# A hybrid decoder step on one core: the first softmax scores of a tile one query feature later

## The chip, the cores and the metric
One Trainium2 chip, one of its cores. The metric is the device time of one execution in microseconds, the median of several runs; lower is better. The engines are TensorE (PE, and PEld for its weight loads), VectorE (DVE), ScalarE (ACT), GpSimd (POOL) and SyncE (SP, which issues the DMAs here).

## The reference
One layer of a decoder with two groups of heads side by side, for a prompt of 2048 tokens and 8 single new tokens. A row norm of x is projected by one combined matrix of width 2832 into:

- a gated linear attention group: 4 heads with keys of 64 and values of 128, a decay from a low-rank gate (rank 16), a per-token recurrence evaluated in chunks;
- a sliding-window softmax group: 8 query heads of width 64 that share 2 key and value heads, window 128, with one learned sink logit per head.

```
proj = einsum('bld,de->ble', rmsnorm(x), w_in)      # gq gk gv g_gate g_low sq sk sv s_gate
o_gla = rmsnorm(gla_scan(gq, gk, gv, log_sigmoid(g_low @ w_gate_up + b) / 16))
s     = q . k / 8, banded: query block i reads key blocks i-1 and i
p     = softmax([s, sink])[..., :-1];   o_swa = p @ v
y     = rmsnorm(x + concat(o_gla * silu(g_gate), o_swa * silu(s_gate)) @ w_out)
```

The outputs are y for the prompt and for the new tokens, the recurrent states, and the last window of keys and values.

## The kernel before, in words
The prompt is cut in 16 tiles of 128 tokens. Every float32 product of the projections is made of three half-precision matmuls (high x high, high x low, low x high; lines L616, L617, L618 in `split_product`). A preamble scales and splits the weights; then a loop over tiles 0 to 14 (`body`) runs on every engine, each with an order written out by hand; tile 15 and the 8 new tokens come behind it. TensorE's body for tile t works ahead: it projects tile t+1 while it finishes the attention of tile t. Tile 0 has an order of its own. The order for t = 1 to 14:

1. `proj(nxt, "sq")`: the window queries of tile t+1, four features of 128 columns, each 8 x 3 matmuls of 128 rows by 128 columns. Between two of them stands `first_scores(t)`, which is `scores(t, 0)`: the scores of units 0 and 1 (12 matmuls of 64 rows, L721).
2. `scores(t, 1)`: units 2 and 3. Then `leaf_scores(t)`, the projection "sklow" (key, value and low-rank part), half of "gv", `values(t, 0)` and `values(t, 1)` (probabilities times values), the rest of "gv", the level scores, `turn_keys`, `turn_low`, `values(t, 2)`, `values(t, 3)`.
3. Part of "gg", the gate, the linear attention's output and state, the rest of "gg", "sg", "gqk" of tile t+2, and the output projection of tile t (L616 to L618 on w_out), with a broadcast `bc(t + 3)` behind its second half's fifth chunk.

PSUM banks are handed out by rings of two. In the ring of the attention each tile fills s0, s1, s2, s3, L1, L2, y0, y1 in turn; a unit waits until the unit two places before it is freed. So s0 and s1 wait for y0 and y1 of the tile before (freed by VectorE's `residual`, L1806), and s2 and s3 wait for s0 and s1, which VectorE frees with the last instruction of `row_max(t, 0)` and `row_max(t, 1)` (L1694 to L1701: two small copies, a predicated copy, two reductions). In the ring of the projections "gv" waits for "sq", which VectorE frees at L1572.

What follows the scores: ScalarE takes the exponential (L1237) and the high half (L1256), VectorE the low half (`rows_lo`, L1719); SyncE then issues a DMA transpose per unit (`turn_prob_rows`, L544), for units 2 and 3 only after TensorE's `values` of units 0 and 1 are over; VectorE masks the transposed tile (`mask_older`, L1725), and `values(t, u)` waits for that. VectorE's order in a tile is row_max 0 and 1, the mean of the final norm (L1812), rows_lo 0 and 1, take_sq (L1572), row_max 2 and 3, mask_older 0 and 1, rows_lo 2 and 3, take_kv, the leaves, the softmax denominators, mask_older 2 and 3, the levels, and then `take_z`, which waits for TensorE.

Of the kernel before, what the change touches and what calls it, by code (L numbers as in the profile page):

```python
# [160 lines left out]
def hymba_step_kernel(nc, xT_d, xq_d, xsT_d, xs_d, w_d, gin_d, gout_d, wgu_d, bg_d, sink_d, normf_d, normfT_d,  # L161
                      state_d, kcT_d, vc_d, sinks_s_d, ident_d, tri_d, lvl_d, leafscan_d, band_d, older_d, window_d,
                      y_d, ys_d, Sp_d, kp_d, vp_d, Ss_d, ksT_d, vs_d):
    with ExitStack() as ctx:
# [446 lines left out]
        def _(pe):  # L611
# [17 lines left out]
            def features(t, bank, at_, c0, ntile, step=P):  # L629

                n = t.tokens
                for f in range(ntile):
                    c = c0 + f * P
                    mm = split_product(bank[:, at_ + f * step:at_ + f * step + n],
                                       [(w_hi[:, d, c:c + P], w_lo[:, d, c:c + P],
                                         u_hi[:, t.p, d, 0:n], u_lo[:, t.p, d, 0:n]) for d in range(DT)])
                return mm

            def rows(t, bank, at_, c0, width, d0=0, d1=DT):

                n = t.tokens
                return split_product(bank[0:n, at_:at_ + width],
                                     [(u_hi[:, t.p, d, 0:n], u_lo[:, t.p, d, 0:n],
                                       w_hi[:, d, c0:c0 + width], w_lo[:, d, c0:c0 + width]) for d in range(d0, d1)],
                                     start=d0 == 0, stop=d1 == DT)

            def proj_rest(t, name, d0, d1=DT):

                mm = rows(t, pj.bank(name, t), 0, COL[name], 512, d0, d1)
                if d1 == DT:  # L650
                    mm.then_inc(pj.full, 1)
# [33 lines left out]
            def proj(t, name, d1=DT, between={}):  # L685
                if t.static and t.off <= 1:
                    i = PREP.index([g for g, _ in GROUPS].index(name))
                    pe.wait_ge(w_lo_done, i + 1)
                pj.wait_free(pe, name, t)
                dve_u.wait(pe, "lo", t)  # L690
                bank = pj.bank(name, t)
                if name in ("gqk", "sq"):
                    for f in range(4):
                        mm = features(t, bank, f * P, COL[name] + f * P, 1)
                        for step, i in between.get(f, ()):
                            step(i)
                elif name == "sklow":
                    features(t, bank, 0, COL[name], 1)
                    mm = rows(t, bank, P, COL[name] + P, P + RANK)
                else:  # L700
                    mm = rows(t, bank, 0, COL[name], 512, 0, d1)
                if d1 == DT:
                    mm.then_inc(pj.full, 1)

            def scores(t, pair):

                units = [f"s{2 * pair + h}" for h in range(KVH)]
                for name in units:  # L710
                    at_ring.wait_free(pe, name, t)
                if pair == 0:
                    pj.wait_freed(pe, "sq", t)
                    pj.wait_freed(pe, "sklow", t)
                    if not (t.static and t.off == 0):
                        win_kept.wait(pe, "win", t + -1)
                for i in range(2):
                    for step, (lq, lk) in enumerate(((0, 0), (0, 1), (1, 0))):
                        for h, name in enumerate(units):
                            r = h * HD  # L720
                            mm = nc.tensor.matmul(at_ring.bank(name, t)[:, i * 2 * P:(i + 1) * 2 * P],  # L721
                                                  q16[r:r + HD, t.p, lq, 2 * pair + i, :], k16[r:r + HD, t.p, lk, :],
                                                  start=step == 0, stop=step == 2)
                            if i == 1 and step == 2:
                                mm.then_inc(at_ring.full, 1)
# [4 lines left out]
            def turn_probs(t, u):  # L730
                name = f"pt{u}"
                tr.wait_free(pe, name, t)
                act_w.wait(pe, f"p{u}", t)
                bank = tr.bank(name, t)
                for i in range(2):
                    tp = nc.tensor.transpose(bank[:, i * P:i * P + P], PR[:, u % 2, i, :], ident[:, :])
                tp.then_inc(tr.full, 1)

            def values(t, u):
                if u == 0:  # L740
                    if t.static and t.off == 0:
                        pe.wait_ge(z_taken, 1)
                    else:
                        dve_o.wait(pe, "sg", t + -1)
                if u == 0:
                    dve_v.wait(pe, "vl", t)
                dve_p.wait(pe, f"k{u}", t)
                h = u % 2
                for i in range(2):
                    c = (u // 2 * 2 + i) * P + h * HD  # L750
                    v = v16[:, t.p, :, h * HD:h * HD + HD]
                    mm = split_product(accS[:, c:c + HD],
                                       [(PT[:, u % 2, m, 0, i, :], PT[:, u % 2, m, 1, i, :], v[:, 2 * m], v[:, 2 * m + 1])
                                        for m in range(2)])
                mm.then_inc(pe_pv.sem, 1)
# [32 lines left out]
            def leaf_scores(t):  # L788

                ring = leaf_ring(t)  # L790
                for h in range(2):
                    ring.wait_free(pe, f"leaf{h}", t)
                dve_g.wait(pe, "leaf", t)
                for f in range(FT):
                    for h in range(2):
                        r = h * DK
                        mm = nc.tensor.matmul(ring.bank(f"leaf{h}", t)[:, f * P:f * P + P],  # L797
                                              EX[r:r + DK, S_LEAFK, f, :], QL[r:r + DK, f, :], start=True, stop=True)
                        if f == FT - 1:
                            mm.then_inc(ring.full, 1)  # L800
# [220 lines left out]
            def body(t):  # L1021
                nxt = t + 1
                early = t.static and t.off == 0
                if early:
                    turn_probs(t, 0)
                    turn_probs(t, 1)
                    scores(t, 1)
                    proj(nxt, "gv")
                    proj(t, "gg")
                    values(t, 0)  # L1030
                    values(t, 1)
                    leaf_scores(t)
                    turn_probs(t, 2)
                    turn_probs(t, 3)
                    proj(t, "sg")
                    values(t, 2)
                    level_scores(t, "L1", 0)
                    values(t, 3)
                    level_scores(t, "L2", 2)
                    turn_keys(t)  # L1040
                    turn_low(t)
                else:
                    proj(nxt, "sq", between={0: [(first_scores, t)]})
                    scores(t, 1)
                    leaf_scores(t)
                    proj(nxt, "sklow")
                    proj(nxt, "gv", 4)
                    values(t, 0)
                    values(t, 1)
                    proj_rest(nxt, "gv", 4)  # L1050
                    level_scores(t, "L1", 0)
                    level_scores(t, "L2", 2)
                    turn_keys(t)
                    turn_low(t)
                    values(t, 2)
                    values(t, 3)
                proj(nxt, "gg", 3)
                gate_up(t)
                gla_out(t)
                state_update(t)  # L1060
                proj_rest(nxt, "gg", 3)
                if early:
                    proj(nxt, "sg", 5)
                    turn_out(t, 0)
                    turn_out(t, 1)
                    proj_rest(nxt, "sg", 5)
                    out_proj(t, 0, 0, 5)
                    bc(t + 2)
                    out_proj(t, 0, 5)
                    out_proj(t, 1)  # L1070
                    proj(t + 2, "gqk")
                    bc(t + 3)
                else:
                    proj(nxt, "sg")
                    proj(t + 2, "gqk")
                    out_proj(t, 0)
                    out_proj(t, 1, 0, 5)
                    if t.n + 3 <= NT:
                        bc(t + 3)
                    out_proj(t, 1, 5)  # L1080

            iterations(pe, body)
            t = Tile(NT - 1)
# [1291 lines left out]
```

## Time and profile before
| | |
|---|---|
| median of 3 runs | 874.51 us (873.07 to 875.18) |
| the profiled execution | 876.44 us, its span 874.7 us |
| TensorE busy (matmuls) | 851.1 us, 97% |
| VectorE, ScalarE, GpSimd busy | 676.9 us, 389.8 us, 77.5 us |
| mean granted TensorE clock | 0.973 |
| one tile of the loop | 48.09 us (scores of tile 2 at 180.92, of tile 3 at 229.01) |

Busy time of an engine is the time in which it has an instruction in work. Matmuls are pipelined and overlap in the records, so their starts say more than their lengths. Where a row ends in brackets, the engine was idle before it for so long and what is named released it.

### The profile page before, as it was taken

To read this page: it belongs to the slowest core of one execution; us is meant where nothing else is said; L and a number is where in the kernel's file an instruction comes from. 1 tells how busy PE (TensorE), PEld (TensorE's weight loads), DVE (VectorE), ACT (ScalarE), POOL (GpSimd) and SP (SyncE) were. 2 spreads that over 40 slices of the span, in tenths; PEclk is the share of its full clock that TensorE was granted. 3 is DMA by queue.
4 is the path that set the end of the run, shared out by engine and by line. 5 is a ranking of instruction groups with operands and counts; after the bars stand their busy time and mean duration, and the time that the engine had idled before them with its cause. 6 is when DMAs were issued, how large, how long until landed. Compare 5 with 4: busy or idle time off the path is not lost.

```text
span 874.7 us, 22036 instructions
## 1 busy us (share of the span) xinstructions
PE 851.1 (97%) x8842; PEld 591.3 (68%) x8842; DVE 676.9 (77%) x2211; ACT 389.8 (45%) x1008; POOL 77.5 (9%) x117
## 2 busy tenths in 40 slices
PE   7898999999999999999999999999999999998997
PEld 5885657676667667576766676675767666764775
DVE  5899787968878787869788787878696887775854
ACT  4556453544444444445444443444454444443411
POOL 0041010101001010101010010101010100101310
PEclk6999999999999999999999999999999999999977
DMA  9922001413122132315132221313141312214033
GB/s 370 394 112 74 25 25 26 121 25 100 35 60 86 38 97 49 99 25 121 25 89 47 60 82 42 97 42 104 27 121 20 110 31 33 63 19 122 3 106 128
DMA packets 75747, 71.22 MB, mean 81 GB/s; under 512 B 63807, under 2 KB 65271, under 8 KB 74622
## 3 DMA queue, kind: packets, MB, share of 16 engines
q1 hardware_dynamic: 75358, 69.75, 27.4%
q8 instruction: 70, 1.15, 0.6%
q14 instruction: 31, 0.25, 0.1%
q10 hardware_dynamic: 288, 0.07, 0.0%
HBM read 44.33 MB, written 10.78 MB: 63 GB/s over the span
## 4 chain that ended last, share of the span: by engine, by line
PE 88%; issue 4%; DVE 4%; DMA 2%; ACT 1%; SPq 0%; POOL 0%; POOLq 0%; DVEq 0%
PE bank L616 25%; PE bank L618 24%; PE bank L617 24%; PE bank L811 3%; PE bank L721 3%; PE bank L670 2%; PE bank L833 2%; PE bank L837 2%; PE bank L848 1%; PE bank L797 1%; DMA w_out_hi<-in_w 1%; DVE w_in_hi_lo L1875 1%; PE bank L626 1%; DMA ogT_lo<-x_rows 1%; DVE xT L1528 0%
## 5 line engine op out<-in xcount | busy, mean ns | idle before, releaser
L616 PE MATMUL bank<-u_hi,w_in_hi_lo 128*128 128x128 f16 (+1 forms) x1288 | 210.3, 215 | 2.9 <-DVE w_in_hi_lo L1875 2.6
L618 PE MATMUL bank<-u_hi,w_in_hi_lo 128*128 128x128 f16 (+1 forms) x1288 | 210.0, 215 | 0.0
L617 PE MATMUL bank<-u_lo,w_in_hi_lo 128*128 128x128 f16 (+1 forms) x1288 | 210.0, 215 | 0.0
L616 PE MATMUL bank<-w_in_hi_lo,u_hi 128*128 128x512 f16 (+3 forms) x528 | 175.1, 341 | 3.6 <-issue 3.6
L618 PE MATMUL bank<-w_in_hi_lo,u_lo 128*128 128x512 f16 (+3 forms) x528 | 175.5, 341 | 0.0
L617 PE MATMUL bank<-w_in_hi_lo,u_hi 128*128 128x512 f16 (+3 forms) x528 | 175.3, 341 | 0.0
L616 PEld LDWEIGHTS bank<-u_hi,w_in_hi_lo 128*128 128x128 f16 x1288 | 124.2, 98 | 12.1 <-issue 3.2
L617 PEld LDWEIGHTS bank<-u_lo,w_in_hi_lo 128*128 128x128 f16 x1288 | 124.1, 98 | 3.0
L618 PEld LDWEIGHTS bank<-u_hi,w_in_hi_lo 128*128 128x128 f16 x1288 | 124.0, 98 | 0.0
L616 PE MATMUL bank<-w_out_hi,ogT_hi 128*128 128x512 f16 x256 | 98.3, 384 | 2.5 <-DMA ogT_lo<-x_rows 2.0
L617 PE MATMUL bank<-w_out_lo,ogT_hi 128*128 128x512 f16 x256 | 98.2, 384 | 0.0
L618 PE MATMUL bank<-w_out_hi,ogT_lo 128*128 128x512 f16 x256 | 98.0, 383 | 0.0
L618 PEld LDWEIGHTS bank<-w_in_hi_lo,u_lo 128*128 128x128 f16 (+1 forms) x528 | 51.6, 98 | 46.9 <-issue 0.8
L616 PEld LDWEIGHTS bank<-w_in_hi_lo,u_hi 128*128 128x128 f16 (+1 forms) x528 | 51.7, 98 | 45.3 <-issue 7.4
L617 PEld LDWEIGHTS bank<-w_in_hi_lo,u_hi 128*128 128x128 f16 (+1 forms) x528 | 51.7, 98 | 38.5 <-issue 0.8
L1237 ACT ACTIVATE flex<-flex,win_stat 128x128 f32<-128x128 f32 x128 | 49.9, 390 | 45.3 <-DVE win_stat L1701 45.3
L1725 DVE TENSOR_TENSOR flex<-flex,older_slot 128x512 f16<-128x512 f16 x56 | 22.7, 423 | 35.1 <-DMA flex<-win_p_rows_hi_lo 35.1
L2228 POOL TENSOR_TENSOR flex<-flex,win_stat 128x512 f32<-128x512 f32 x16 | 16.7, 1043 | 372.3 <-DVE win_stat L1737 345.9
L1296 ACT ACTIVATE ogT_hi<-flex 128x1024 bf16<-128x1024 f32 x16 | 16.9, 1056 | 73.3 <-DVE flex L1806 73.3
L1701 DVE CUSTOM_DVE_ANT_0 flex<-bank,band_bf,neg_sinks 128x128 f32<-128x128 f32 x128 | 47.0, 405 | 0.0
L618 PEld LDWEIGHTS bank<-w_out_hi,ogT_lo 128*128 128x128 f16 x256 | 25.3, 99 | 31.0 <-issue 1.4
L616 PEld LDWEIGHTS bank<-w_out_hi,ogT_hi 128*128 128x128 f16 x256 | 25.8, 101 | 29.8 <-issue 4.3
(310 smaller groups left out, 1663.7 us busy)
## 6 DMA issues: line engine op xcount, KB each, us to landing
xT<-in_xT SPq DMA_DIRECT2D x16, 512.0 KB, 3.3
x_rows<-in_xq SPq DMA_DIRECT2D x16, 512.0 KB
flex<-in_w SPq DMA_DIRECT2D x4, 2048.0 KB, 9.9
flex<-in_xq SPq DMA_DIRECT2D x16, 512.0 KB, 4.1
out_y<-flex SPq DMA_DIRECT2D x16, 512.0 KB, 3.7
w_out_lo<-in_w SPq DMA_DIRECT2D x2, 2048.0 KB, 11.9
w_out_hi<-in_w SPq DMA_DIRECT2D x1, 2048.0 KB, 9.9
w_out_hi<-in_w SPq DMA_DIRECT2D x1, 1088.0 KB, 7.5
```

Of the source, the lines that this page charges most:

```text
L616: nc.tensor.matmul(out, a_hi, b_hi, start=start and i == 0, stop=False)
L617: nc.tensor.matmul(out, a_hi, b_lo, start=False, stop=False)
L618: mm = nc.tensor.matmul(out, a_lo, b_hi, start=False, stop=stop and i == last)
L670: mm = nc.tensor.matmul(out[0:w, 0:w], top[:, d, c:c + w], top[:, d, c:c + w], start=d == 0 and c == 0, stop=d == DT - 1 and (c, w) == blo ...
L721: mm = nc.tensor.matmul(at_ring.bank(name, t)[:, i * 2 * P:(i + 1) * 2 * P], q16[r:r + HD, t.p, lq, 2 * pair + i, :], k16[r:r + HD, t.p, l ...
L811: mm = nc.tensor.matmul(bank[:, c:c + P], EX[:, l0 + l, f, :], QE[:, l0 + l, f].rearrange("p h c -> p (h c)"), start=True, stop=True)
L833: nc.tensor.matmul(accG[:, f * 2 * DV:(f + 1) * 2 * DV], EX[:, S_INTER, f, :], S_bd[:, f].rearrange("p h c -> p (h c)"), start=f == 0, sto ...
L837: mm = nc.tensor.matmul(accG[:, h * DV:h * DV + DV], AT[:, h, :], gv[:, t.p, h * DV:h * DV + DV], start=False, stop=h == HG - 1, skip_grou ...
L1237: e = nc.scalar.activation(PR[:, u % 2, i, :], PR[:, u % 2, i, :], ACT.Exp, scale=-1.0, bias=wst[:, 0, k:k + 1], accum_out=wst[:, 1, k:k + 1])
L1296: nc.scalar.activation(junk[0:n, :], xres[0:n, :], ACT.Square, accum_out=hst[0:n, 0:1]).then_inc(act_o.sem, 1)
L1701: m = V.tensor_tensor_reduce(PR[:, u % 2, i, :], bank[:, i, P:2 * P], band[:, first], nsig[:, :], nsink[:, k:k + 1], ALU.add, ALU.min, wst ...
L1725: V.tensor_tensor(PT[:, u % 2, 1].rearrange("p l h c -> p (l h) c"), PT[:, u % 2, 0].rearrange("p l h c -> p (l h) c"), bcast(older16[:, : ...
```

## The change
`first_scores(t)` moves from behind feature 0 to behind feature 1 of the next tile's query projection, in tiles 1 to 14 on TensorE. No other engine's order changes and no instruction is added or dropped. The broadcast behind five chunks of the output projection is in both kernels.

```diff
@@ -1040,7 +1040,7 @@
                     turn_keys(t)
                     turn_low(t)
                 else:
-                    proj(nxt, "sq", between={0: [(first_scores, t)]})
+                    proj(nxt, "sq", between={1: [(first_scores, t)]})
                     scores(t, 1)
                     leaf_scores(t)
                     proj(nxt, "sklow")
```

## Rows read from the trace of the kernel before

**Rows 1.** The page, part 1: busy us, share of the span, instructions.
```profile
PE 851.1 (97%) x8842; PEld 591.3 (68%) x8842; DVE 676.9 (77%) x2211; ACT 389.8 (45%) x1008; POOL 77.5 (9%) x117
```

**Rows 2.** The waits of TensorE: us in total, times, longest.
```profile
PE bank L616 <- issue: 3.6, 1, 3.6
...
PE bank L721 <- DVE flex L1806: 1.0, 1, 1.0
...
PE bank L616 <- ACT gla_k L1164: 0.3, 1, 0.3
```

**Rows 3.** The chain that ended last, tiles 2 and 3: start, us.
```profile
180.92 0.76 PE bank L721 x12
...
229.01 0.76 PE bank L721 x12
```

**Rows 4.** Timeline of TensorE's weight loads, tile 6, from 373.3 us.
```profile
373.40 0.10 PEld L618 LDWEIGHTS bank<-u_hi,w_in_hi_lo 128*128 128x128 f16 x1
373.60 0.55 PEld L721 LDWEIGHTS bank<-win_k_hi_lo,win_q_hi_lo 64*128 64x128 f16 x12
...
374.44 0.10 PEld L618 LDWEIGHTS bank<-u_hi,w_in_hi_lo 128*128 128x128 f16 x1
...
378.29 0.10 PEld L618 LDWEIGHTS bank<-u_hi,w_in_hi_lo 128*128 128x128 f16 x1
378.49 0.55 PEld L721 LDWEIGHTS bank<-win_k_hi_lo,win_q_hi_lo 64*128 64x128 f16 x12
```

**Rows 5.** Timeline of VectorE, tile 6, from 369 us.
```profile
372.58 0.74 DVE L1806 SCALAR_TENSOR_TENSOR flex<-bank,row_unscale,flex 128x512 f32<-128x512 f32 x1
374.47 0.15 DVE L1694 COPY win_stat<-neg_sinks 128x1 f32<-128x1 f32 x1 [1.14 <-PE bank L721]
...
376.64 0.41 DVE L1701 CUSTOM_DVE_ANT_0 flex<-bank,band_bf,neg_sinks 128x128 f32<-128x128 f32 x1
...
379.35 0.69 DVE L1572 SCALAR_TENSOR_TENSOR win_q_hi_lo<-bank,win_q_hi_lo 128x512 f16<-128x512 f32 x1 [0.39 <-ACT win_q_hi_lo L1180]
...
382.45 0.76 DVE L1725 TENSOR_TENSOR flex<-flex,older_slot 128x512 f16<-128x512 f16 x2
...
384.01 0.42 DVE L1719 SCALAR_TENSOR_TENSOR win_p_rows_hi_lo<-flex,win_p_rows_hi_lo 128x256 f16<-128x256 f32 x1 [0.47 <-ACT win_p_rows_hi_lo L1256]
...
388.11 0.42 DVE L1725 TENSOR_TENSOR flex<-flex,older_slot 128x512 f16<-128x512 f16 x1 [1.42 <-DMA flex<-win_p_rows_hi_lo]
389.43 0.42 DVE L1725 TENSOR_TENSOR flex<-flex,older_slot 128x512 f16<-128x512 f16 x1 [0.90 <-DMA flex<-win_p_rows_hi_lo]
```

**Rows 6.** Timeline of all engines at tile 15's first scores, behind the loop.
```profile
806.10 0.75 DVE L1806 SCALAR_TENSOR_TENSOR flex<-bank,row_unscale,flex 128x512 f32<-128x512 f32 x1 [4.42 <-PE bank L618]
...
806.92 0.14 PEld L721 LDWEIGHTS bank<-win_k_hi_lo,win_q_hi_lo 64*128 64x128 f16 x4 [1.45 <-DVE flex L1806]
```

**Rows 7.** Timeline of all engines at the second scores of tile 14.
```profile
761.75 0.41 DVE L1701 CUSTOM_DVE_ANT_0 flex<-bank,band_bf,neg_sinks 128x128 f32<-128x128 f32 x1
...
763.61 0.12 PEld L721 LDWEIGHTS bank<-win_k_hi_lo,win_q_hi_lo 64*128 64x128 f16 x4
```

**Rows 8.** Timeline of TensorE's matmuls, tile 6, from 378 us.
```profile
382.55 0.38 PE L616 MATMUL bank<-w_in_hi_lo,u_hi 128*128 128x512 f16 x1
...
385.14 0.19 PE L616 MATMUL bank<-win_v_hi_lo,flex 128*128 128x64 f16 x1
...
385.49 0.19 PE L616 MATMUL bank<-win_v_hi_lo,flex 128*128 128x64 f16 x1
...
390.84 0.19 PE L616 MATMUL bank<-win_v_hi_lo,flex 128*128 128x64 f16 x1
```

**Rows 9.** The waits of VectorE and of SyncE's queue.
```profile
DVE flex L1725 <- DMA flex<-win_p_rows_hi_lo: 35.1, 30, 2.5
DVE win_stat L1694 <- PE bank L721: 16.2, 15, 1.2
...
SPq L544 <- PE bank L618: 33.2, 14, 2.4
```

## The prediction, made before the result was known
> **What bounds the kernel now.** I read the page first. TensorE has work in 97% of the span, VectorE in 77% and ScalarE in 45% [rows 1]. So a change inside the tile loop costs or gives only what it does to TensorE's idle time. The view of waits then says where TensorE is idle. It has 13 kinds of wait; the longest is 3.6 us and the shortest 0.3 us, and together they make 3.6 + 2.6 + 2.0 + 2.0 + 1.9 + 1.4 + 1.1 + 1.0 x 4 + 0.5 + 0.3 = 19.4 us. The only one on the line of the scores (L721) is 1.0 us [rows 2], and it lies at 806.9 us, where tile 15 is scored behind the loop [rows 6], a place that the change does not touch. In the chain of work the scores of every tile stand on TensorE, and the first ones repeat every 48.09 us (180.92, then 229.01) [rows 3]. The loop's tiles are therefore TensorE's own work from end to end, and there is no stall in them at the scores that a change of place could remove.
>
> **What the change does on TensorE.** Nothing is added, removed or resized. In tiles 1 to 14, feature 1 of the next tile's query (24 matmuls with their weight loads) now runs before the first scores instead of after them. A feature's loads go from 374.44 to 378.29 in 69 steps, 0.0558 us each, so a feature is 24 x 0.0558 = 1.34 us [rows 4]. There is a small toll at each entry from the features to the scores: from the last load of the features (373.40) to the first load of the scores (373.60) it is 0.20 us where the cadence is 0.056, so 0.14 us more; the same at the second entry (378.29 to 378.49) [rows 4]. There are two such entries per tile before and two after, so the toll stays. TensorE's busy sum changes by 0.
>
> **The wait that moves nearer.** The second scores (units s2, s3) start at a place that doesn't move, but they write the two banks that VectorE frees with row_max(t,0) and row_max(t,1), and these can only start when the first scores are there, now 1.34 us later. I followed tile 6. The last reduction of row_max(t,1) starts at 376.64 and takes 0.41, so it ends at 377.05 [rows 5]; the second scores' first load is at 378.49 [rows 4]. That is 1.44 us of cover. The first and the last tile of the loop that have it (tiles 1 and 14) show the same; tile 14's row_max ends at 761.75 + 0.41 = 762.16 against 763.61, which is 1.45 [rows 7]. VectorE was idle for 1.14 us ahead of row_max(t,0), waiting for TensorE [rows 5], so it follows the scores directly and the whole 1.34 us passes on: the end becomes 378.39. How long from there until TensorE starts? At tile 15 the bank was really waited for: VectorE's L1806 ended at 806.10 + 0.75 = 806.85 and the first load started at 806.92, 0.07 later [rows 6]. So the load could start at 378.39 + 0.07 = 378.46, and TensorE wants it at 378.49. The cover is 0.03 us per tile. I put the cost at 0, with bounds of 0 and, if my three roundings all go against me, some 0.03 us x 14 = 0.4 us. Queued behind this wait on TensorE are the leaf scores, the key, value and low-rank projection and all that follows; a late release would push all of it, undiluted.
>
> Between the two entries, the toll of 0.14 us in front of the second scores is what hides the last of the lateness: the release at 378.46 comes after 378.35, when the next load would come at the cadence, but before 378.49. The Trainium skill, TensorEngine Tiling (Array Packing), section Tiling Modes, says that changing the tiling mode drains TensorE, and these scores change from 128 to 64 rows; by it the toll runs while the release is awaited, the cost is 0 as above, and if the drain began only at the release it would be the rival A below. The trace shows the toll, and not which of the two begins it.
>
> **What is late next.** ScalarE's exponentials, VectorE's low halves, and the first two DMA transposes of the probabilities all follow row_max and come 1.34 us later. The next fixed places on TensorE's side:
> values(t,0) starts at 385.14 [rows 8]; its mask is the first of two that start at 382.45 and take 0.76 together [rows 5], so both end at 383.21, then 384.55: 0.59 us to spare even for the second.
> The query's bank must be free before the value projection at 382.55 [rows 8]; VectorE's L1572 ends at 379.35 + 0.69 = 380.04, then 381.38: 1.17 to spare.
> The third and fourth transposes need TensorE's values(t,0) and values(t,1) to be over, as well as VectorE's low halves. SyncE waits there for TensorE in all 14 tiles, 33.2 us in total, 2.37 each [rows 9]. The low half of unit 3 ends at 384.01 + 0.42 = 384.43, then 385.77 [rows 5], about when values(t,1), which starts at 385.49, is through [rows 8], and unit 2's transpose is issued first. So these two stay where TensorE puts them. VectorE's mask of unit 2 waits 1.42 us for its DMA (388.11) [rows 5]; this becomes 1.42 - 1.34 = 0.08 us, and here the shift is eaten. Behind this point VectorE is back on its old times, and nothing reaches the next tile. The values of unit 3 at 390.84 [rows 8] stay covered: the mask of unit 3 ends at 389.43 + 0.42 = 389.85 as before.
>
> Upside at the first scores: they need y's second bank, freed at 372.58 + 0.74 = 373.32 [rows 5], plus 0.07 = 373.39, and start at 373.60. They are not held, so their new place gives 0.
>
> **Sum.** Profiled execution: 876.44 us, of which 874.7 is span. Change 0 + 0 + 0, so 876.4 in that execution. The three timed runs have the median 874.51 (873.07 to 875.18), 1.9 below the profiled one; on their scale the forecast is 874.6, the 0.1 for a few hundredths in some tiles. A change under 0.3% (2.6 us, or 0.19 us in each of 14 tiles) is about what a measurement of this kernel cannot tell from none.
>
> **Rivals.**
> A, the toll comes after the wait. If the 0.14 us begins only once the banks are free, the second scores start at 378.46 + 0.14 = 378.60, 0.11 late: 14 x 0.11 = 1.5 us, 876.1. For it: nothing in this trace shows a late release ahead of a change of shape. Against it: in tile 15 the load came 0.07 after the release, but with the array already empty [rows 6]. Even doubled, 0.20 x 14 = 2.8 us (877.3) only touches the limit.
> B, slower: the fourth transpose follows VectorE and not TensorE. If the chain to unit 3's mask moved by the full 1.34, that mask would end at 389.85 + 1.34 = 391.19 and with 0.07 release values(t,3) at 391.26 against 390.84: 0.42 x 14 = 5.9 us, 880.4. It decides from 0.19 us per tile, that is, once unit 3's mask ends 1.11 us later than now. Against it: the 2.37 us that SyncE waits for TensorE is more than 1.34 [rows 9], so the cover is real, though for unit 3 only thin (385.77 against about 386.0).
> C, faster: the 0.20 us ahead of the first scores is in truth a late release of y's bank. Then one feature more hides it: 14 x 0.14 = 2.0 us, 872.5. Against it: the same 0.20 us stands ahead of the second scores, whose banks had been free for 1.44 us [rows 4, 5].
>
> **How the numbers follow.** Forecast (between 0 and 0.05 us per tile) 0.73; A 0.14; B 0.08; C 0.05. Forecast, A and C lie within 0.3%, but the three timed runs lie over 2 us apart, so I give 0.04 to faster, 0.86 to same and 0.10 to slower (B and the upper end of A). The range goes from 873.0, C's side with the spread of the runs, to 877.3, the upper bound of A. B alone is left out above it.
>
> **What the profile after should show.** The first scores 2.68 us instead of 1.34 after the query's start, and 3.55 us between the two groups' starts instead of 4.89 (378.49 - 373.60) [rows 4]. VectorE's idle ahead of L1694 rises from 16.2 to about 16.2 + 14 x 1.34 = 35 us; its idle for the transposed probabilities (L1725) falls from 35.1 to about 35.1 - 18.8 = 16 us; SyncE's wait for TensorE at L544 falls from 33.2 to about 14 us [rows 9]. TensorE shows no wait, or hundredths, of L721 for L1701. I am wrong if L721 waits for L1701 with more than 0.19 us per tile, if L616 to L618 wait for L1725, or if the period of 48.09 us changes.

## The result and the profile after

| | before | changed |
|---|---|---|
| median of 21 timed runs | 875.1 us (871.28 to 876.75) | 877.32 us (871.68 to 878.41) |
| the profiled execution, its span | 876.44 us, 874.7 us | 871.68 us, 869.8 us |
| mean granted clock in it | 0.973 | 0.981 |

The ratio is 1.0029, interval 1.0017 to 1.0040: slower by 0.3%, clear of its interval. "Same" (under 0.3%) had the chance 0.86; 877.32 lies 0.02 us above the range, which ends at 877.3. One execution of the kernel before, in the series of E0, took 1351 us at a mean granted clock of 0.592 and is left out of all that follows.

The profiled execution of the changed kernel is 4.8 us shorter than that of before, although the kernel is slower. The view of windows, for the tile loop and for the end, says why; its columns are the stretch, its length, busy us and instructions of PE, PEld, DVE, ACT and POOL, granted clock, DMA share, GB/s. Before:

```profile
132.00:757.00 625.00, 624.77 (x6269) 425.99 (x6267) 498.60 (x1668) 283.69 (x778) 46.29 (x78) 1.00 0.26 66
832.00:875.00 43.00, 35.97 (x394) 27.37 (x393) 20.20 (x70) 5.80 (x23) 1.59 (x3) 0.74 0.33 116
```

Changed:

```profile
132.00:757.00 625.00, 624.81 (x6260) 426.79 (x6257) 505.64 (x1664) 284.50 (x779) 46.57 (x78) 1.00 0.26 66
832.00:875.00 43.00, 29.71 (x369) 22.29 (x365) 19.50 (x69) 4.48 (x16) 0.40 (x1) 0.84 0.30 105
```

The second stretch runs past the end of both spans (874.7 and 869.8 us). In the loop both have the full clock; at the end one execution was granted 0.74 and the other 0.84. So two single executions can't be compared by their spans, and the loop has to be read by itself. There, the chain of work of the changed kernel, tiles 2 and 3 (start, us):

```profile
179.55 0.76 PE bank L721 x12
183.10 0.82 PE bank L721 x12
...
227.69 0.76 PE bank L721 x12
231.24 0.81 PE bank L721 x12
```

The period, the time from the first scores of one tile to those of the next, is 227.69 - 179.55 = 48.14 us against 48.09 [rows 3], and the second scores take 0.81 or 0.82 instead of 0.76. The loss is in every tile and it is at the second scores. It can be read over the whole loop too: from the first scores of tile 1 to those of tile 14, 13 periods, it is 625.5 to 626.0 us in the three profiled executions with the order of before (before, before again, E7; mean 625.72) and 626.2 to 626.6 in the four of the changed kernel (mean 626.37). The difference of 0.65 is 13 x 0.05. Each of these seven executions also has one to four periods that are 0.1 to 0.4 us longer than the rest; what makes them so was not followed.

The view of waits shows what moved. The forecast was 35, 16 and 14 us:

```profile
DVE win_stat L1694 <- PE bank L721: 35.0, 15, 2.6
...
DVE flex L1725 <- DMA flex<-win_p_rows_hi_lo: 8.1, 10, 1.2
...
SPq L544 <- PE bank L618: 14.4, 14, 1.2
```

but it has no line of TensorE that waits at L721 for L1701: the delay is too small for it. It must be read from the starts. All engines in tile 6 of the changed kernel:

```profile
372.30 0.83 PE L721 MATMUL bank<-win_k_hi_lo,win_q_hi_lo 64*128 64x256 f16 x12
...
375.34 0.41 DVE L1701 CUSTOM_DVE_ANT_0 flex<-bank,band_bf,neg_sinks 128x128 f32<-128x128 f32 x1
...
375.64 0.10 PEld L618 LDWEIGHTS bank<-u_hi,w_in_hi_lo 128*128 128x128 f16 x1
...
375.67 0.08 DVE L1701 DVE_READ_ACCUMULATOR2_ANT win_stat<- 128x1 f32 x1
...
375.87 0.58 PEld L721 LDWEIGHTS bank<-win_k_hi_lo,win_q_hi_lo 64*128 64x128 f16 x12
375.90 0.83 PE L721 MATMUL bank<-win_k_hi_lo,win_q_hi_lo 64*128 64x256 f16 x12
```

The last reduction of row_max(t,1) ends at 375.34 + 0.41 = 375.75. It is not the last row of row_max, as I had described it: behind it stands the read-out of its maximum into win_stat, also of L1701, which ends at 375.67 + 0.08 = 375.75 as well; the view of waits names `DVE win_stat L1701` as releaser where the wait is long enough to be listed (E3). The first load of the second scores starts 0.12 us later, at 375.87; it would have started at 375.64 + 0.20 = 375.84 [rows 4]. In the four profiled executions of the changed kernel this distance is 0.11 to 0.13 us in each of the 14 tiles. The first matmul follows the load by 0.03, at 375.90, as at tile 15, where the load is at 806.92 [rows 6] and the matmul at 806.95; not held, in tile 6 of before, both stand at 378.49. The load is late by 0.03 or a little less and the matmul behind it by 0.03 more: 0.05 us a tile. From the first matmul of the first scores to the first of the second it is 3.60 us.

What was to be late next is not. VectorE's masks of units 2 and 3:

```profile
385.51 1.75 DVE L1725 TENSOR_TENSOR flex<-flex,older_slot 128x512 f16<-128x512 f16 x2
```

They end at 387.26, 11.39 us after the second scores' first load (375.87); before it was 389.85 - 378.49 = 11.36 [rows 4, 5]. The row merges the two masks with the DMA wait between them, 1.75 - 2 x 0.42 = 0.91 us. In 9 of the 14 tiles they stand merged like this. The 9 x 0.91 = 8.2 us that the view of waits doesn't count and its 8.1 us make the 16 of the forecast.

### The profile page after: what moved, and what is told of

It reads as the page before. It is cut to its first block, busy times and chain, and to the rows that moved or that the text cites. A ratio compares the mean times of both kernels' runs of the same rounds, so it can differ in the third digit from the quotient of the medians.

```text
span 869.8 us, 22036 instructions
## 1 busy us (share of the span) xinstructions
PE 844.2 (97%) x8842; PEld 587.1 (67%) x8842; DVE 683.9 (79%) x2211; ACT 389.6 (45%) x1008; POOL 77.9 (9%) x117
## 4 chain that ended last, share of the span: by engine, by line
PE 88%; DVE 5%; issue 4%; DMA 2%; ACT 1%; SPq 0%; POOL 0%; POOLq 0%; DVEq 0%
PE bank L616 25%; PE bank L617 24%; PE bank L618 24%; PE bank L811 3%; PE bank L721 3%; PE bank L833 2%; PE bank L837 2%; PE bank L670 1%; DVE w_in_hi_lo L1875 1%; PE bank L848 1%; PE bank L797 1%; DMA w_out_hi<-in_w 1%; PE bank L626 1%; DMA ogT_lo<-x_rows 1%; DVE xT L1528 0%
## 5 line engine op out<-in xcount | busy, mean ns | idle before, releaser
L1701 DVE CUSTOM_DVE_ANT_0 flex<-bank,band_bf,neg_sinks 128x128 f32<-128x128 f32 x128 | 47.0, 405 | 0.0
L1528 DVE SCALAR_TENSOR_TENSOR xT<-xT,u_gain,bank 128x128 f32<-128x128 f32 (+1 forms) x136 | 35.6, 333 | 12.2 <-PE bank L626 12.2
```

What stands on the lines that cost most here:

```text
L1528: u = V.scalar_tensor_tensor(out=xT[:, d, 0:n], in0=xT[:, d, 0:n], scalar=ugain[:, d:d + 1], in1=pj.bank("bc", t)[:, 0:n], op0=ALU.mult, o ...
L1701: m = V.tensor_tensor_reduce(PR[:, u % 2, i, :], bank[:, i, P:2 * P], band[:, first], nsig[:, :], nsink[:, k:k + 1], ALU.add, ALU.min, wst ...
```

## The experiments

Theory 1: only the release of the two score banks counts; it reaches TensorE after 0.12 us and is just late. Its rivals are that the place of the first scores costs by itself (theory 2), and, for the part of the measured loss that the loop doesn't show, that the change makes the granted clock fall more often (theory 3) or that this is chance (theory 4). Each run gives its span and its mean granted clock. Over the 232 executions of all kernels here for which both are recorded, a fit with one offset for each kernel and one slope for the clock gives -0.65 us for each +0.001 of mean clock. "At equal clock" below is the offset of such a fit over the kernel before. It leaves 0.63 us of scatter, where the spans of before alone scatter by 1.7. The +- is the standard error of the fit over all series; it doesn't contain what differs from one series to another (the changed kernel's own four series, below, differ by more). The diffs are against the changed kernel.

**E0, the changed kernel again.**

> The changed kernel once more, as the yardstick of this series. In its first profile the second scores start 0.03 to 0.05 us late in each tile and the period is 48.14 us against 48.09, 0.7 us in 14 tiles, while its 21 timed runs have a median 2.2 us above the kernel before. Theory 1 (the late release of the two score banks is all of it, and the rest of the 2.2 us is the clock that a single execution happened to be granted outside the loop): ratio between 1.000 and 1.003, and a profile whose span is near 875 us with the same period of 48.14 us. Theory 2 (timed executions lose more in the loop than that one profile shows): ratio 1.003, and a second profile shows a period of 48.2 us or more.

Measured: ratio 1.0028 (1.0015 to 1.0041), median 877.04; in its profile the span is 874.6 and the period 48.14 (180.63, then 228.77). The loss repeats, and so does the 0.05 us per tile, no more. Theory 2 as worded in this expectation (a longer period in another execution) falls.

**E1, half a feature.** A feature may now be cut between two of its 8 chunks; the lines that do the cutting are left out here, as in E4 and E5.

```diff
-                    proj(nxt, "sq", between={1: [(first_scores, t)]})
+                    proj(nxt, "sq", between={1: [(first_scores, t)]}, split={1: 4})
```

> First scores behind feature 0 and the first half (4 of 8 chunks) of feature 1, so 0.67 us later than before and 0.67 us earlier than in the changed kernel. Theory 1 (only the release of the banks that the second scores write counts, with 0.03 us of cover left at a whole feature): 0.70 us of cover, period 48.09 us as before, ratio 1.000. Theory 2 (the time follows the place of the first scores, by way of the later VectorE, ScalarE and DMA work or the clock): about half of the loss, ratio 1.0013.

Measured: ratio 0.9999 (0.9981 to 1.0017), at equal clock +0.03 +- 0.19 us, period 48.08 (181.23, then 229.31). The release comes 0.75 to 0.77 us before the load in every tile. Half of the move costs nothing, as theory 1 has it.

**E2, the leaf scores first.**

```diff
+                    leaf_scores(t)
                     scores(t, 1)
-                    leaf_scores(t)
                     proj(nxt, "sklow")
```

> The changed kernel with the leaf scores (8 matmuls, 0.5 us) ahead of the second scores instead of behind them: first scores where the change puts them, and 0.5 us more between the groups. Theory 1: the release comes 0.4 us before it is wanted, the period is 48.09 us again, ratio 1.000. Theory 2: the place of the first scores is unchanged, so the loss of the changed kernel stays, ratio 1.0025.

Measured: ratio 1.0010 (0.9994 to 1.0025), but at equal clock +1.64 +- 0.19 us, and the period is 48.18 (180.95, then 229.13). My expectation missed. Its rows in tile 6:

```profile
377.21 0.10 PEld L618 LDWEIGHTS bank<-u_hi,w_in_hi_lo 128*128 128x128 f16 x1
...
377.23 0.09 DVE L1701 DVE_READ_ACCUMULATOR2_ANT win_stat<- 128x1 f32 x1
...
377.85 0.65 PEld L721 LDWEIGHTS bank<-win_k_hi_lo,win_q_hi_lo 64*128 64x128 f16 x12
...
377.96 0.82 PE L721 MATMUL bank<-win_k_hi_lo,win_q_hi_lo 64*128 64x256 f16 x12
...
378.71 0.10 PEld L616 LDWEIGHTS bank<-u_hi,w_in_hi_lo 128*128 128x128 f16 x1 [0.21 <-issue]
```

and one of the kernel before, the first load behind its leaf scores:

```profile
379.70 0.10 PEld L616 LDWEIGHTS bank<-u_hi,w_in_hi_lo 128*128 128x128 f16 x1
```

VectorE is through at 377.23 + 0.09 = 377.32, 0.53 us before the load at 377.85, so the second scores are not held any more, as theory 1 has it. But from the last load of the query features to the first load behind the two groups it is 378.71 - 377.21 = 1.50 us, where before it was 379.70 - 378.29 = 1.41 [rows 4]. The order itself costs TensorE 0.09 us a tile, more than the late release that it removes, so the times of this run decide nothing between the theories. Why this order (float32 matmuls of 64 rows ahead of float16 ones) is dearer is not shown.

**E3, two features more than before.**

```diff
-                    proj(nxt, "sq", between={1: [(first_scores, t)]})
+                    proj(nxt, "sq", between={2: [(first_scores, t)]})
```

> First scores behind feature 2, one more than in the change. Theory 1: cover of 0.03 us minus 1.34 us, so the second scores wait for the banks some 1.35 us in each of 14 tiles, visible as a wait of L721 for L1701 of some 19 us, period 49.4 us, ratio 1.0215. Theory 2 (a loss per feature of the size of the measured one): 2.2 us more, ratio 1.005.

Measured: ratio 1.0208 (1.0185 to 1.0231), at equal clock +19.8 us, period 49.47 (182.31, then 231.78). Its view of waits has TensorE at L721 behind L1701 14 times:

```profile
PE bank L721 <- DVE win_stat L1701: 18.5, 14, 1.3
```

Its timeline of TensorE's matmuls in tile 6:

```profile
380.39 0.83 PE L721 MATMUL bank<-win_k_hi_lo,win_q_hi_lo 64*128 64x256 f16 x12
...
383.99 0.83 PE L721 MATMUL bank<-win_k_hi_lo,win_q_hi_lo 64*128 64x256 f16 x12 [1.32 <-DVE win_stat L1701]
```

and of the weight loads:

```profile
383.96 0.25 PEld L721 LDWEIGHTS bank<-win_k_hi_lo,win_q_hi_lo 64*128 64x128 f16 x6 [1.46 <-DVE win_stat L1701]
```

From group to group it is 3.60 us, as in the changed kernel, though a feature less stands between them: both are set by VectorE. Its last reduction here starts at 383.43 and takes 0.41, and from 383.84 to the load at 383.96 it is 0.12 us again, now with the loads idle for 1.46 us. It is 0.12 or 0.11 in all 14 tiles. So this is the way from the end of row_max to the load, whether TensorE's last matmul is still in work at the release (in the changed kernel it starts at 375.70) or over for more than a us. Rival A wanted the 0.14 us of toll after the release; in the changed kernel the load would then have come later than on an idle TensorE. It came after the same 0.12.

**E5, one and a quarter features.**

```diff
-                    proj(nxt, "sq", between={1: [(first_scores, t)]})
+                    proj(nxt, "sq", between={2: [(first_scores, t)]}, split={2: 2})
```

> First scores behind feature 1 and a quarter (2 of 8 chunks) of feature 2, 0.335 us later than in the changed kernel. Theory 1: past the end of the cover every further us is paid in full, so 0.05 + 0.335 = 0.385 us per tile, period 48.48 us, 5.4 us in all, ratio 1.006; the wait of L721 for L1701 is visible in each tile. A theory of a cost per move that does not depend on the release gives ratio 1.003.

Measured: ratio 1.0058 (1.0035 to 1.0081), at equal clock +5.34 +- 0.22 us against 5.4 expected; period 48.49 (180.21, then 228.70); and from group to group 3.60 us again (374.82 to 378.42), with the load 0.11 or 0.12 us behind row_max's end in every tile.

**E4, seven eighths of a feature.** As E1, with `split={1: 7}`.

> First scores behind feature 0 and seven of eight chunks of feature 1, so 0.17 us earlier than in the changed kernel. Theory 1: the cover is 0.15 us more, the 0.05 us per tile are gone, period 48.09 us, ratio 1.000 and, if the clock goes with the small wait (theory 3), the clock of before. If instead the clock or the time goes with the place of the first scores, the ratio is that of the changed kernel, 1.0025.

Measured: ratio 1.0001 (0.9990 to 1.0012), at equal clock +0.20 +- 0.19 us, period 48.10 (180.47, then 228.57). The load is 0.25 to 0.27 us behind the release, so it isn't held. One chunk of 0.17 us earlier and the loss is gone. Its mean clock, 0.9759 against 0.9766 of before on that chip, did not come back with it.

**E6, a shorter row_max.** Everything on TensorE stays as changed.

```diff
-                V.tensor_copy(wst[:, 3, u:u + 1], nsink[:, u:u + 1])
                 V.copy_predicated(bank[:, :, P:2 * P], bcast(older[:, :].bitcast(I32), 1, 2), bank[:, :, 0:P]
```

> The changed kernel without the first of the two small copies in row_max (L1694, on every tile and unit; nothing reads what it writes before the second copy writes it again). The places on TensorE stay as the change has them; only VectorE's chain between the two groups of scores gets shorter, by about 0.07 us per row_max, 0.13 us in two. Theory 1 (only the release of the banks counts): the second scores are no longer late, the distance of the two groups is 3.55 us with the toll of before, period 48.09 us, and at equal clock 0 to 0.2 us over before instead of 1.0. If the place of the first scores itself costs, the 48.14 us and the 1.0 us stay.

Measured: ratio 0.9991 (0.9973 to 1.0009), at equal clock +0.03 +- 0.20 us, period 48.09 (180.60, then 228.69). TensorE's matmuls in tile 6:

```profile
372.89 0.83 PE L721 MATMUL bank<-win_k_hi_lo,win_q_hi_lo 64*128 64x256 f16 x12
...
376.44 0.83 PE L721 MATMUL bank<-win_k_hi_lo,win_q_hi_lo 64*128 64x256 f16 x12
```

The groups are 3.55 us apart, which is what the changed order takes on TensorE when it is not held, 0.05 less than the 3.60 of the changed kernel.

The release comes 0.21 or 0.22 us before the load. This is the cleanest of the runs: the first scores are where the change puts them, VectorE is 0.13 us faster between the two groups, and the loss is not there. The place does not cost; the release does.

**E7, the same copy left out of the kernel before.**

> The same copy left out of the kernel before, as the control: there the release has 1.44 us of cover, so all theories expect ratio 1.000 and the period of 48.09 us.

Measured: ratio 1.0004 (0.9986 to 1.0022), at equal clock +0.10 +- 0.19 us, period 48.09 (178.16, then 226.25). With 1.44 us of cover a faster row_max gives nothing.

**Before against itself, and the changed kernel twice more.**

> The kernel before, run as if it were a changed one, for the size of a difference of nothing. All theories: ratio 1.000 within its interval. It also tells how often this kernel gets the higher granted clock: so far 7 of 28 executions of before had a span under 871 us at a mean granted clock of 0.979 or more, and 1 of 33 of the changed kernel.

> The changed kernel a third time, on another chip perhaps. Theory 1 (0.05 us per tile, because the load follows the release after 0.12 us here and not 0.07, so 0.7 us; the rest is a lower granted clock outside the loop): at equal mean clock 0.7 to 1.3 us longer than before; period 48.14 us. Theory 3 (the change itself makes the clock fall more often): again hardly an execution with a mean clock of 0.979 or more, and a mean clock 0.002 under that of before. Theory 4 (the clock is chance): mean clocks of this and before within 0.0005, and a ratio of 1.0008 to 1.0015.

> The changed kernel again, for the granted clock. Theory 3 (the change makes the clock fall more often): mean clock of its executions 0.0015 under that of before on this chip too. Theory 4 (chance): within 0.0005. At equal clock both expect 1.0 us over before.

Measured: before against itself 0.9991 (0.9977 to 1.0005), so a difference of nothing shows up to 0.1% off; the changed kernel 1.0014 (0.9996 to 1.0032) and 1.0018 (0.9998 to 1.0039), periods 48.15 and 48.14. All 57 executions of the changed kernel with a recorded clock lie 0.99 +- 0.11 us over the 101 of before at equal clock. Its four series one by one give 0.93, 1.46, 0.65 and 0.86, each +- 0.15 to 0.18: they differ by more than these errors, and the last two agree with the 0.7 us of the periods.

As to the clock, the mean is 0.9755 for the changed kernel against 0.9768. In the three series that recorded both it is 0.9754 against 0.9769, 0.9758 against 0.9766 and 0.9763 against 0.9770: each time lower, and only the first by twice its uncertainty. By the slope, 0.0013 is 0.85 us. Theory 3 expected 0.002 and then 0.0015, theory 4 within 0.0005; the second and third series lie between. Theory 3 had a second expectation, that the changed kernel would again hardly ever be granted 0.979 or more, as in 1 of its first 33 executions. That failed: in the last two series it was 6 of 24, where before had 19 of 73. Nor does the clock go with the move in the other kernels: it is 0.979 in E3 and 0.9776 in E5, which move the scores further and wait longer, and 0.9782 in E6, with the place of the change. This speaks for chance, but the lower mean of the changed kernel stays unexplained.

## Why the prediction was wrong, point by point

Two of its own signs decide it. TensorE was to show "no wait, or hundredths", which came true, and the prediction was to be wrong "if the period of 48.09 us changes": it is 48.14, and the second scores are held in every tile. That the median lies outside the range as well is luck: the same kernel's other three medians, 877.04, 876.37 and 876.51, lie inside it, with the same loss in the loop.

What bounds the kernel, and that the first scores were not held before: right. Nothing was gained there: with the wait for the banks out of the way (E1, E4, E6) the period is 48.08 to 48.10 us, that of before, so rival C is out.

A feature of 1.34 us, passed on whole to row_max and all behind it: right. VectorE's idle ahead of L1694 rose to 35.0 us as forecast, and the order leaves 3.55 us between the two groups (E6).

The cover. This is the step that failed, as a size: "How long from there until TensorE starts?" was answered with 0.07 us, from the one held start of scores in the trace, at tile 15, where TensorE was held by another VectorE instruction (L1806). That row was read rightly; there it is 0.07 or 0.08 in the profile of every run. But at the second scores in the loop it is 0.12 us, in the changed kernel, in E5 and in E3. With 0.12 the load comes at 378.39 + 0.12 = 378.51 against 378.49: 0.02 late instead of 0.03 early. To this comes a term that the sum did not have: held, the first matmul follows its load by 0.03 us. The cost is 0.05 us x 14 = 0.7 us where I had 0 to 0.4. I had measured a cover of 1.44 us in rows good to 0.01 us and then decided about a remainder of 0.03 with a latency from one other place.

What makes it 0.12 here stays open. It is not the releasing instruction: in the trace of before, behind the loop, the leaf scores wait for the same read-out of L1701,

```profile
819.60 0.08 DVE L1701 DVE_READ_ACCUMULATOR2_ANT win_stat<- 128x1 f32 x1
...
819.75 0.55 PEld L797 LDWEIGHTS bank<-flex 64*128 64x128 f32 x8 [0.56 <-DVE win_stat L1701]
```

and their load comes 819.75 - 819.68 = 0.07 us behind it. It is not the entry to 64 rows either, which both places with 0.07 share, nor the idle time before it (E3). One difference was not tried: in the loop VectorE's next instruction, L1812, follows the read-out at once (375.67, 0.15 us long) and ends 0.05 us ahead of the load, while at 819.68 VectorE pauses for 0.04 us. So no row of the trace of before gave the 0.12.

The cover's slope, seen from both sides: no cost at half a feature (E1), 0.2 +- 0.2 at seven eighths (E4), 1.0 at one (changed), 5.3 at one and a quarter (E5), 19.8 at two (E3), in us at equal clock. From the edge on each us of delay is paid once per tile, 14 times; 0.335 x 14 = 4.7 more from one to one and a quarter against 5.34 - 0.99 = 4.35.

What is late next: right. SyncE's wait for TensorE shrank to 14.4 us and did not vanish, unit 3's mask ends at its old distance, and rival B is out.

Rival A: its total (1.5 us) is not far from what was measured at equal clock, but its mechanism is not the one; the toll runs while the release is awaited. The load came 0.12 us after the release in the changed kernel and in E3 alike. The Trainium skill (TensorEngine Tiling (Array Packing), Tiling Modes) says that a change of the tiling mode drains TensorE. The 0.20 us at the entry from 128 rows to 64 [rows 4], where the cadence is 0.056, is compatible with that; that it is a drain, the trace doesn't show.

The rest of the 2.2 us between the medians. At equal clock the change costs 0.99 +- 0.11 us, of which the period explains 0.7. About 0.3 us is not placed; with series that range from 0.65 to 1.46 it may be nothing. The remaining part of the difference of the medians, some 1.2 us, goes with the lower mean clock of the changed kernel's executions: in these 21 it was 0.9749, 0.0019 under before's 0.9768 in the other series, and that is 1.2 us by the slope. It is not shown that the change causes it.

The base. I took 874.51, the median of three runs; over 21 runs it is 875.1. That is 0.6 of the 2.7 us by which 874.6 missed. Three runs out of a spread of 5 us were too few for a range whose upper end was to decide within a tenth of a us.

## What to carry to other kernels

When an instruction is moved towards one that waits for it through another engine, the number to know is the shortest time of that loop: here 3.60 us from the first scores through two row_max and back (E3, E5), against the 3.55 us of TensorE's own work that the new order leaves between them (E6). With the two so close, neither a sum of rounded rows nor the view of waits decides; stay a chunk of work away from the edge, which costs nothing here (E4 and E1). The latency of a release is no constant, not even for one releasing instruction (0.07 us at 819.75, 0.12 in the loop, both behind L1701): where the cover that is left is smaller than this difference of 0.05, the bound must have room for it. And a loop's loss is read from its period, since single spans differed here by 5 us through the clock alone.

## What the runs showed of the hardware that I had not expected

The way from VectorE's release to TensorE's weight load was 0.07 us behind L1806 at tile 15 and behind L1701 at 819.75, and 0.12 us behind L1701 in the loop. Behind a release the first matmul of the scores stood 0.03 us after its load, where without a wait, behind a feature, both started together (378.49). In E2, without a wait but behind the float32 leaf scores, it was 0.11 us (377.85, then 377.96).

The mean granted clock of an execution ranged from 0.972 to 0.984 over the 232 executions of all these kernels, and in the profiled ones the loop had 1.00, so that the differences lie at the beginning and the end. It goes with 0.65 us for each 0.001 and explains most of the scatter of the times. Comparing the executions at equal clock shows a difference of 1 us that the medians alone blur.
